# Router scratch over dead activations, the tenth expert place filled with the first ones, and the last expert transfer in two pieces

## The reference

```python
def _expert_choice_moe(h, router_w, w_gate, w_up, w_down):
    b, t, d = h.shape                                   # 1, 256, 1024
    capacity = CAPACITY_FACTOR * t // N_EXPERTS         # 32 tokens for each of 16 experts
    logits = jnp.einsum('btd,de->bte', h, router_w).astype(jnp.float32)
    affinity = jax.nn.softmax(logits, axis=-1)
    gate, idx = lax.top_k(jnp.swapaxes(affinity, 1, 2), capacity)
    xe = jax.vmap(lambda hb, ib: hb[ib])(h, idx)
    hidden = jax.nn.silu(jnp.einsum('becd,edf->becf', xe, w_gate)) * jnp.einsum('becd,edf->becf', xe, w_up)
    ye = jnp.einsum('becf,efd->becd', hidden, w_down) * gate[..., None].astype(h.dtype)
    return jax.vmap(
        lambda ib, yb: jnp.zeros((t, d), yb.dtype).at[ib.reshape(-1)].add(yb.reshape(-1, d))
    )(idx, ye)
```

## Time and profile before

| | us |
|---|---|
| three runs | 1948.5, 1946.1, 1948.7 (median 1948.5) |
| the profiled run | 1948.7 |
| its span, first to last instruction | 1946.9 |
| PE busy | 1517.2 (78%) |
| DVE busy | 625.5 (32%) |
| ACT busy | 529.9 (27%) |
| mean granted TensorE clock | 0.885 of full |

### The profile page before, as it was taken

How to read it: one execution, slowest core, us unless ns; L and a number is a source line. 1 busy time by engine, 2 the same in 40 slices (tenths; PEclk the granted TensorE clock), 3 DMA queues, 4 the chain that set the end, 5 groups by cost and what they waited for, 6 DMA issues and landing times.

```text
span 1946.9 us, 25845 instructions
## 1 busy us (share of the span) xinstructions
PE 1517.2 (78%) x11156; PEld 1031.7 (53%) x11174; DVE 625.5 (32%) x980; ACT 529.9 (27%) x868; POOL 134.0 (7%) x151
## 2 busy tenths in 40 slices
PE   7999999999999997899888665566555566555665
PEld 7888999887999897789463111121111112111211
DVE  5665445666454544445761000000000000000000
ACT  6455443545434456425631000000000000000000
POOL 0351000031000013410200000000000000000000
PEclk9999999999999989999989777867878878778776
DMA  8443555433555443213098999999999999999997
GB/s 268 153 142 130 173 183 183 152 133 128 182 185 192 121 127 115 84 48 130 7 382 345 427 429 428 427 429 427 428 428 428 428 428 428 427 428 428 427 428 305
DMA packets 138561, 542.01 MB, mean 278 GB/s; under 512 B 10093, under 2 KB 103490, under 8 KB 113890
## 3 DMA queue, kind: packets, MB, share of 16 engines
q1 hardware_dynamic: 138418, 540.50, 70.7%
q0 software_dynamic: 48, 0.13, 0.0%
HBM read 539.56 MB, written 1.05 MB: 278 GB/s over the span
## 4 chain that ended last, share of the span: by engine, by line
PE 46%; DMA 43%; DVE 5%; ACT 3%; POOL 2%; issue 1%; SPq 0%; DVEq 0%; ACTq 0%; POOLq 0%
DMA ew<-in_expert_w_up_dram 14%; DMA ew<-in_expert_w_gate_dram 14%; DMA ew<-in_expert_w_down_dram 14%; PE bank L1082 11%; PE bank L1083 11%; PE bank L1084 11%; PE bank L1577 2%; PE bank L1600 1%; PE bank L1089 1%; DVE wL L1621 1%; POOL arena L671 1%; PE bank L1103 1%; PE bank L1166 1%; PE bank L1305 1%; ACT wH L714 1%
## 5 line engine op out<-in xcount | busy, mean ns | idle before, releaser
L1577 PE MATMUL bank<-ew,xeT 128*32 128x512 f32 x2048 | 340.2, 799 | 236.5 <-DMA ew<-in_expert_w_up_dram 128.3
L1621 DVE TENSOR_TENSOR wL<-ring,wH 128x2048 fp32r<-128x2048 f32 x128 | 294.8, 2303 | 273.5 <-ACT wH L714 273.2
L1577 PEld LDWEIGHTS bank<-ew,xeT 128*32 128x32 f32 x2048 | 64.5, 129 | 495.5 <-DMA ew<-in_expert_w_up_dram 210.4
L714 ACT ACTIVATE wH<-ring 128x2048 fp32r<-128x2048 f32 x128 | 244.4, 1910 | 286.5 <-PE bank L1084 284.1
L1082 PE MATMUL bank<-xH,wH 128*128 128x256 f32 x1056 | 303.9, 288 | 7.6 <-DVE wL L1621 7.0
L1083 PE MATMUL bank<-xL,wH 128*128 128x256 f32 x1056 | 300.2, 284 | 0.0
L1084 PE MATMUL bank<-xH,wL 128*128 128x256 f32 x1056 | 300.1, 284 | 0.0
L1600 PE MATMUL bank<-ew,tok 128*32 128x256 f32 x2048 | 173.0, 497 | 103.0 <-DMA ew<-in_expert_w_down_dram 95.4
L1082 PEld LDWEIGHTS bank<-xH,wH 128*128 128x128 f32 x1056 | 203.8, 193 | 14.3 <-issue 9.0
L1083 PEld LDWEIGHTS bank<-xL,wH 128*128 128x128 f32 x1056 | 203.9, 193 | 0.8
L1084 PEld LDWEIGHTS bank<-xH,wL 128*128 128x128 f32 x1056 | 203.8, 193 | 0.0
(11 more groups left out here) (287 smaller groups left out, 1785.3 us busy)
## 6 DMA issues: line engine op xcount, KB each, us to landing
ew<-in_expert_w_gate_dram SPq DMA_DIRECT2D x64, 2048.0 KB, 46.1
ew<-in_expert_w_up_dram SPq DMA_DIRECT2D x64, 2048.0 KB, 46.0
ew<-in_expert_w_down_dram SPq DMA_DIRECT2D x64, 2048.0 KB, 46.6
ring<-in_w_gate_up_dram SPq DMA_DIRECT2D x44, 1024.0 KB, 5.1
ring<-in_w_down_dram SPq DMA_DIRECT2D x22, 1024.0 KB, 4.9
ring<-in_w_in_dram SPq DMA_DIRECT2D x22, 1024.0 KB, 5.3
ring<-in_w_out_dram SPq DMA_DIRECT2D x12, 1024.0 KB, 4.9
ring<-in_w_in_fox_dram SPq DMA_DIRECT2D x10, 1024.0 KB, 9.6
```

The source lines that it names most:

```text
L714: act.activation(wH[:, n % 2, w], ring[:, slot(n), w], ACT.Copy).then_inc(w_hi, 1)
L1577: mm = pe.matmul(bank[half][32 * j:32 * j + 32, :], xeT[:, k, CAP * e:CAP * e + CAP], w_[:, m, 512 * j:512 * j + 512], start=(k == 0), sto ...
L1621: dve.tensor_tensor(wL[:, n % 2, w], ring[:, slot(n), w], wH[:, n % 2, w].bitcast(F32), ALU.subtract).then_inc(w_split, 1)
```

## The change

Four edits.

1. The router's scratch leaves the memory under place 9. `top8`, `logitsT` and `affT` lie in the second 256 columns of `xeT`'s chunks 0 to 3, `sel` in those of chunks 4 to 7 (over the parts of `xH` and `xL` that the router product has read by then). `diag` of "ffn2" lies in `gate_hi`. The squares of "ffn2" on ACT write their unused output to `tok`.
2. Place 9 is loaded with the first group, as g = 3. The places of g = 4 to 9 are those of g = 3 to 8 before, behind the same waits. After that g waits for `e_used` g - 9 throughout.
3. The last transfer (g = 191) is issued as two of 1 MB, each with half of the columns of each partition (8 KB). PE waits for the second (`e_rest`) in front of the second half of the last 16 matmuls.
4. `wf_parts` and `wr_parts` become one semaphore, `thin_parts` (waits for 1 and 2, and then for 3 and 4).

```diff
-            sel, bias_sb = shared("sel", [P, NT, NE, CAP], F32R, "bias_sb", [P, 4, S], F32, front)
+            bias_sb = fsb("bias_sb", [P, 4, S])
...
-        xeT = sb("xeT", [P, KD, NE * CAP])
+        xeT_r, xeT = shared("xeT_r", [P, KD, NE * CAP], F32R, "xeT", [P, KD, NE * CAP], F32)
...
-        top8 = s_sb[0:NE, 0, 0:CAP].rearrange("p (r c) -> p r c", c=8)
-        affT = p_sb[0:NE, 0:3, :]
-        logitsT = s_sb[0:NE, 1, :]
+        late = xeT[:, :, S:2 * S]
+        top8 = late[0:NE, 0, 0:CAP].rearrange("p (r c) -> p r c", c=8)
+        affT = late[0:NE, 1:4, :]
+        logitsT = late[0:NE, 0, :]
+
+        def sel(part, t):
+
+            return xeT_r[:, 4 + NT * part + t, S:2 * S]
...
-        def diag(t):
-
-            return pT_sb[:, t, 0, 0:P]
+        def diag(t, name=None):
+
+            return gate_hi[:, 0, P * t:P * t + P] if name == "ffn2" else pT_sb[:, t, 0, 0:P]
...
-        EORDER = (0, 1, 2, 5, 3, 4, 6, 7, 8, 9)
-
-        FIRST = ESLOTS - 1
+        EORDER = (0, 1, 2, 9, 5, 3, 4, 6, 7, 8)
+        LAST = NE * EU - 1
 
         def eslot(g):
-            return EORDER[g if g < FIRST else (g - FIRST) % ESLOTS]
+            return EORDER[g % ESLOTS]
 
         def e_landed(g):
 
-            return 16 if g < FIRST else 16 * ((g - FIRST) // ESLOTS + 1 + ((g - FIRST) % ESLOTS < FIRST))
+            return 16 * (g // ESLOTS + 1)
...
-                sp.dma_start(ew[:, eslot(g), :], src).then_inc(e_full[eslot(g)], 16)
+                if g < LAST:
+                    sp.dma_start(ew[:, eslot(g), :], src).then_inc(e_full[eslot(g)], 16)
+                    return
+                for part in range(2):
+                    c = slice(EW // 2 * part, EW // 2 * part + EW // 2)
+                    sp.dma_start(ew[:, eslot(g), c], src[:, c]).then_inc((e_full[eslot(g)], e_rest)[part], 16)
 
             dif = att_base["dif"]
             sp.wait_ge(att["pv"], dif["pv"] + 16)
-            for g in range(3):
+            for g in range(4):
                 load_expert(0, g)
             sp.wait_ge(w_split, NU - 4)
-            load_expert(0, 3)
+            load_expert(0, 4)
             sp.wait_ge(sn_ss, 4)
             sp.wait_ge(mTL, 4)
-            load_expert(0, 4)
+            load_expert(0, 5)
             sp.wait_ge(w_split, NU)
-            load_expert(0, 5)
             load_expert(0, 6)
+            load_expert(0, 7)
             sp.wait_ge(w_used, NU)
-            load_expert(0, 7)
             load_expert(0, 8)
-            for g in range(FIRST, NE * EU):
-                if g == 2 * FIRST:
-                    sp.wait_ge(xe_mm, 2 * KD)
-                else:
-                    sp.wait_ge(e_used, g - FIRST + 1 if g < 2 * FIRST else g - ESLOTS + 1)
+            load_expert(0, 9)
+            for g in range(ESLOTS, NE * EU):
+                sp.wait_ge(e_used, g - ESLOTS + 1)
                 load_expert(g // EU, g % EU)
...
-                    square(src, i, i, scratch(i)).then_inc(nrm["sq"], 1)
+                    square(src, i, i, piece(tok, i) if name == "ffn2" else scratch(i)).then_inc(nrm["sq"], 1)
...
-                                           sel[:, t, e0:e0 + NE // 2, :].rearrange("p e c -> p (e c)"),
+                                           sel(part_, t),
...
                     for m in range(4):
+                        if e * EU + 8 + j == LAST and m == 2:
+                            pe.wait_ge(e_rest, 16)
                         for q in range(4):
```

More of the change, by code:

```diff
@@ L234, in build @@
         tokL = [t_[:, :, :].rearrange("p a b -> p (a b)") for t_ in (hidH, hidL)]
-        def diag(t):
-            return pT_sb[:, t, 0, 0:P]
+        def diag(t, name=None):
+            return gate_hi[:, 0, P * t:P * t + P] if name == "ffn2" else pT_sb[:, t, 0, 0:P]
         full = [sem(f"full{i}") for i in range(RING)]
         e_full = [sem(f"e_full{i}") for i in range(ESLOTS)]
+        e_rest = sem("e_rest")
         w_hi = sem("w_hi")
@@ L337, in lay_at @@
             return L * LAY_ADDS[k] + v
-        wf_parts = sem("wf_parts")
+        thin_parts = sem("thin_parts")
         ang_step = sem("ang_step")
@@ L364, in build @@
             "ro_mm", "ro_v", "ro_e", "ro_tr", "ro_key", "ro_kt", "sel_ok", "xe_mm", "xe_ev", "xe_evd"))
-        wr_parts, ro_lt = sem("wr_parts"), sem("ro_lt")
+        ro_lt = sem("ro_lt")
         pg_ok, pg_tr, pgT_ok, e_sg, e_hid, e_hTm, e_hT, e_y, e_cmb, e_add, out_done = (
@@ L821, in _ @@
                     act.wait_ge(small_in, 16 * N_SMALL)
-                    act.activation(wfH, wf, ACT.Copy).then_inc(wf_parts, 1)
+                    act.activation(wfH, wf, ACT.Copy).then_inc(thin_parts, 1)
                 product(n)
@@ L1005, in _ @@
             act.wait_ge(kr_mm, 1)
-            act.activation(wrH, wr[:, :, :], ACT.Copy).then_inc(wr_parts, 1)
+            act.activation(wrH, wr[:, :, :], ACT.Copy).then_inc(thin_parts, 1)
             dn = (dn_sq, dn_ss, dn_rms)
@@ L1103, in transposes @@
                             mm = pe.matmul(b2(first + b)[:, j, P * t:P * t + P], src[:, t, P * k:P * k + P],
-                                           diag(t), start=True, stop=True)
+                                           diag(t, name), start=True, stop=True)
                         if t == NT - 1:
@@ L1334, in _ @@
                 if L == 0:
-                    pe.wait_ge(wf_parts, 2)
+                    pe.wait_ge(thin_parts, 2)
                     pe.wait_ge(mem_ev, 3)
@@ L1528, in _ @@
             normed("ffn2")
-            pe.wait_ge(wr_parts, 2)
+            pe.wait_ge(thin_parts, 4)
             for k in range(KD):
@@ L1550, in gather @@
                 pe.wait_ge(sel_ok, 2 * part_ + 2)
-                e0 = NE // 2 * part_
                 for k in range(KD):
@@ L1634, in root @@
                 dve.wait_ge(nrm["rstd"], norm_at(name, "rstd", t + 1))
-                dve.tensor_scalar(diag(t), ident[:, :], rstd[:, t:t + 1], None, ALU.mult).then_inc(nrm["diag"], 1)
+                dve.tensor_scalar(diag(t, name), ident[:, :], rstd[:, t:t + 1], None, ALU.mult).then_inc(nrm["diag"], 1)
             def loaded_roots(name):
@@ L1821, in _ @@
                 if j == 3:
-                    dve.wait_ge(wf_parts, 1)
-                    dve.tensor_tensor(wfL, wf, wfH.bitcast(F32), ALU.subtract).then_inc(wf_parts, 1)
+                    dve.wait_ge(thin_parts, 1)
+                    dve.tensor_tensor(wfL, wf, wfH.bitcast(F32), ALU.subtract).then_inc(thin_parts, 1)
                 low(n + 2)
@@ L2034, in _ @@
                         head_scale(which, (dq_tok, dk_tok)[which], t, dn_mul, HD)
-            dve.wait_ge(wr_parts, 1)
-            dve.tensor_tensor(wrL, wr[:, :, :], wrH.bitcast(F32), ALU.subtract).then_inc(wr_parts, 1)
+            dve.wait_ge(thin_parts, 3)
+            dve.tensor_tensor(wrL, wr[:, :, :], wrH.bitcast(F32), ALU.subtract).then_inc(thin_parts, 1)
             dve.wait_ge(lam_ok, 2)
@@ L2143, in choose @@
                 for t in range(NT):
-                    dve.tensor_tensor(sel[:, t, es, :], keyt[:, t, es].rearrange("p (e a) -> p e a", a=1)
+                    dve.tensor_tensor(sel(part, t).rearrange("p (e c) -> p e c", c=CAP), keyt[:, t, es].rearrange("p (e a) -> p e a", a=1)
                                       .broadcast_to([P, NE // 2, CAP]),
```

## The result

Six executions of each kernel: 1940.1 us median after (1936.1 to 1940.9), 1947.5 before (1945.1 to 1948.7), ratio 0.9958 with an interval of 0.9946 to 0.9970. A second series gave 0.9964 (0.9950 to 0.9978). By the two intervals the change makes the kernel faster by 0.2 to 0.5%. The gain forecast was 7.2 us, from 1948.5 to 1941.3; the first series says 8.2 us (5.8 to 10.5), the second 7.0.

What follows compares the result with a forecast made beforehand. The expert-weight DMA stream was taken to bound the kernel's last half. Profiled span 1946.9 - 4.9 (tenth place) - 2.3 (split last transfer) = 1939.7, plus 1.8 around it, less 0.2 to the median: 1941.3 us; range 1939.5 to 1944.3.

Steps and rivals of the forecast that it cites:

- Bound by the stream: Expert stage: 192 weight transfers, one per 4.90 us, set its length; PE waits for data; the restart time counts fully.
- The tenth place: Expert loads before the restart: ten instead of nine, leaving 182 transfers instead of 183 after it; minus 4.9 us.
- The two steps on the way: Expert loads before the restart: five issues instead of four at 971.2 us, and no DMA shortfall at 998.
- The last transfer: Kernel's end: with two pieces PE goes from unit 190 straight into 191; minus 2.3 us, bounds 1.0 and 2.5.
- the slower of two rows: Last two units: clock rises 4.8 us after unbroken PE work begins, as in the filler; the other row had about 3.
- The rival with the low clock to the end: Last two units: clock stays low throughout, gain 1.0 us instead of 2.3, time 1942.6 us; chance 26%.
- The pieces: Last transfer: one more issue and 8 KB runs instead of 16 KB cost nothing; 1.4 us kept for the range.
- the rival of 2 us: Last transfer: the second piece pays a fixed cost of about 2 us on the path, time 1943.3 us; chance 8%.
- The edits at nothing: Router scratch, ffn2 squares and merged semaphore: same instructions in the same order, no waits lengthened; 0 us.
- The rival of the slower restart: Restart: DVE's top-32 chain stretches beyond 0.8 us of cover, PE idles, clock may be low; 1950.1 us, chance 4%.
- The level: Whole kernel: the starting time of 1948.5 us, median of three runs that reach from 1946.1 to 1948.7.
- the lower end: Range's lower end, 1939.5 us: gain of 2.5 at the end, quick last units, run low in the 2.6 us spread.

Runs made afterwards that it cites:

- tenth_only: The kernel after the change, but with the last transfer in one piece: scratch moved and tenth place filled early; ratio to before 0.9963.
- split_only: The kernel before with only the last transfer in two pieces and the thin weights' two semaphores made one; ratio to before 0.9993.
- late_restart: The kernel after, with the first three transfers of the restart held until PE has used three units, not one; ratio to before 0.9987.
- moves_only: The kernel after with the old order of loads and the last transfer whole, so only the router's scratch is moved; ratio to before 1.0003.
- the early unit: The kernel after, with the first unit of expert 0 put between the two halves of gather(0); ratio to before 0.9966.
- tail_filler: The kernel after, with filler matmuls on zeros in PE's idle time in front of units 189 and 190; ratio to before 0.9968.

## Why the prediction was right or wrong

**Bound by the stream: right.** Every us at the restart was one at the end, both ways (3.43 gave 3.28, 1.96 gave 1.6), and near the end PE waited for DMA in front of every unit but the first of the last expert's down matrix (0.69 us for ACT in after), which it made up before the next.

**The tenth place, 4.9 us: right.** 4.6 to 4.95 by the marks (tenth_only, after); with every profile of the old stream against every one of the new, 4.3 to 5.1. The two steps on the way came as told: five issues in the first group and no shortfall at 998. The idle stretch was some 9 us, as reckoned (9.3).

**The last transfer, 2.3 us: the mechanism right, the size off in this kernel.** It measured 1.7 in both profiles of after, 2.3 in split_only, and lies inside the bounds of 1.0 and 2.5. What failed in this term is the moment of the clock's rise: I took the slower of two rows, 4.8 us after the start of unbroken work, and in the two profiles of after it was 6.0 and 5.9. In late_restart, whose last units began at the low clock too, it was 2.7. So the start of unbroken work doesn't tell the moment, and two rows were no bound. The rival with the low clock to the end (a gain of 1.0) was in no profile; after fell between it and the forecast, and the profiles with 6.5 at the forecast. That 2.3 came out in split_only is in part luck: the clock was low for three of its last microseconds too, at a time when it cost nothing.

**The pieces: right to take at nothing** (0.07 us), and the rival of 2 us falls.

**The edits at nothing: right.** moves_only is before, in the ratio and in the marks. The rival of the slower restart falls with it and with 58.65 to 58.70 us in every kernel whose restart wasn't touched.

**The level, and with it the lower end: wrong.** This is the step of the sum that failed. The sum of the terms measured 6.6 us by the marks against 7.2, so the gain wasn't under-estimated. What was mis-sized is the time it was taken from, 1948.5: before's six runs of the same series had the median 1947.5. The forecast is 2.0 us above the 1939.3 of the first series; 1.0 of that is this level, and 1.0 is that the ratio gives a gain of 8.2 and not 7.2. The sum was made against one profile and the median of three runs (1948.5), and I held both for typical, since they agreed. That profile had both slow places in the dense stages, 3.1 us together. Later series of the same kernel had medians of 1946.4, 1945.2 and 1946.6, so that the level is 1.0 to 3.3 us below the one I took. The range's low end allowed for "the lower part of the spread of 2.6 us", the spread of those three runs; later ones reached from 1943.0 to 1950.2 in one series. The low end should have been some 2 us lower for that alone (an estimate: half of 7.2 - 2.6). The larger gain by the first ratio (8.2 us) is within its interval of the 6.6 that the marks show; nothing in the traces needs the other 1.6, and what they are stays open.

## What to carry to other kernels

Where a stage is one saturated stream of transfers, its length is the time of its restart plus a count: a transfer that is moved into the idle time ahead of the restart is worth a full period, and each us by which the first place comes free is worth about one (the early unit gave 1.6 to 1.9 more for four lines). Split the last transfer, not all: that split saved 0.85 to 2.3 us, by the clock over the last unit, and the split of every one cost 12.5.

When effects are smaller than the spread between executions, look for marks inside the traces that repeat (here from the first expert load to unit 190, to some tenths of a us) and compare those; and don't set the end of a range by the spread of three runs.

## What the runs showed of the hardware that I had not expected

- A good part of the spread of a one-core kernel came in steps, from three places. At one, an idle time of PE of 2.9 us, the clock was at 0.50 for some microseconds behind it in some executions and at 1.00 throughout in others, worth 1.5 or 2.6 us there. The other two were worth 1.5 us each. The rest, up to 3.1 us, arose without steps in the first 75 us.
- The rise from 0.50 to 1.00 came 2.7 us (the last units of late_restart), 3 us (the last unit before), 4.8 us (the filler before) and 6 us (the last units after) after the start of unbroken work.
- Halving a queued transfer of 2 MB, from 16 KB to 8 KB runs, cost 0.07 us of 4.90, 1.4%; the page's rate fell from 428 to 421 GB/s.
- The stream has four places in each profile at which a unit comes about 1.5 us late, 207 to 227 us apart in after, and 212 to 222 in before. And for some 6 us at the end only half of the DMA engines' time is used, and less after that: in tail_filler from 1922 on, 9 us before the last landing, as in this window:

```profile
1924.00:1925.00 1.00, 0.98 (x5) 0.25 (x3) 0.00 (x0) 0.00 (x0) 0.00 (x0) 1.00 0.54 229
```

Four times 1.5 us is about that last stretch, so some of the engines may be the ones delayed; neither what the delays are nor this was tested.
